# A two-block network on one NeuronCore: branch products over four PSUM banks, and the 96-slot expert pass written in line

## The reference

```python
def gated_mixer(h, w_in, ...):
    proj = h @ w_in
    gates = jax.nn.sigmoid(proj[..., o0:] + b_gate).reshape(B, S, 2, D)
    out_a = diff_attention(qa, ka, va, lam, lam_init, subln_w)
    out_b = chunk_band_attention(qb, kb, vb, rel_bias)
    merged = gates[:, :, 0] * (out_a @ w_branch_a) + gates[:, :, 1] * (out_b @ w_branch_b)
    return merged @ w_out

def moe_ffn(h, w_router, b_router, w_exp_in, b_exp_in, w_exp_out, b_exp_out):
    logits = t @ w_router + b_router
    top_val, top_idx = lax.top_k(logits, TOP_K)          # 4 of 32 experts per token
    gate_w = jax.nn.softmax(top_val, axis=-1)
    # for each expert, on the tokens that chose it:
        hb = xb @ w_exp_in[e] + b_exp_in[e]
        g = jnp.minimum(hb[:, :D_FF_2], 7.0); u = jnp.clip(hb[:, D_FF_2:], -7.0, 7.0)
        a = g * jax.nn.sigmoid(1.702 * g) * (u + 1.0)
        y = a @ w_exp_out[e] + b_exp_out[e]
```

## Time and profile before

| | before |
|---|---|
| median of three runs | 1506.52 us |
| profiled execution: device time | 1507.34 us |
| profiled execution: span, first to last instruction | 1505.5 us |
| around the span | 1.84 us |
| PE busy | 1339.8 us (89%) |
| VectorE busy | 448.4 us (30%) |
| ScalarE busy | 359.8 us (24%) |
| instructions executed | 25303 |

### The profile page before, as it was taken

One profiled execution on the slowest core, in us unless ns is written; L12 is line 12 of the kernel. 1 busy time (PEld: TensorE's weight loads), 2 busy tenths in 40 slices (PEclk: granted clock), 3 DMA queues, 4 the chain that ended last, 5 costly groups with the idle time before them and its releaser, 6 DMA issues.

```text
span 1505.5 us, 25303 instructions
## 1 busy us (share of the span) xinstructions
PE 1339.8 (89%) x9344; PEld 801.1 (53%) x9345; DVE 448.4 (30%) x906; ACT 359.8 (24%) x690; POOL 139.0 (9%) x65
## 2 busy tenths in 40 slices
PE   7999999998999898988998888998889988889865
PEld 6454999887989863434343333343334333433432
DVE  1326677745543771111111111111011111111112
ACT  1234666545566520101000100010001001000101
POOL 0000122005765400000000000000000000000000
PEclk9999999999999999999999999999999999999997
DMA  9442466855344478999999999999999999999996
GB/s 342 152 129 56 118 190 181 320 195 187 135 147 168 168 285 364 429 425 427 424 411 426 429 426 426 424 412 425 427 424 428 411 425 426 428 428 424 407 427 258
DMA packets 113493, 494.35 MB, mean 328 GB/s; under 512 B 7617, under 2 KB 55089, under 8 KB 80465
## 3 DMA queue, kind: packets, MB, share of 16 engines
q1 hardware_dynamic: 111971, 491.50, 81.5%
q10 hardware_dynamic: 1486, 2.34, 0.4%
HBM read 492.76 MB, written 1.06 MB: 328 GB/s over the span
## 4 chain that ended last, share of the span: by engine, by line
PE 59%; DMA 33%; DVE 3%; ACT 2%; issue 2%; SPq 0%; DVEq 0%; ACTq 0%
DMA big_mem<-in_w_exp_in 29%; PE ps L953 16%; PE ps L994 6%; PE ps L696 5%; PE ps L698 5%; PE ps L697 5%; PE ps L524 4%; PE ps L936 4%; DMA big_mem<-in_w_exp_out 3%; PE ps L668 2%; PE ps L720 1%; PE ps L722 1%; PE ps L721 1%; PE ps L1017 1%; PE ps L513 1%
## 5 line engine op out<-in xcount | busy, mean ns | idle before, releaser
L953 PE MATMUL ps<-big_mem,ring_mem 128*32 128x512 f32 (+1 forms) x2304 | 382.4, 640 | 67.7 <-DMA big_mem<-in_w_exp_in 67.7
L953 PEld LDWEIGHTS ps<-big_mem,ring_mem 128*32 128x32 f32 (+1 forms) x2304 | 112.6, 125 | 313.2 <-issue 200.8
L994 PE MATMUL ps<-big_mem,x 128*32 128x256 f32 (+1 forms) x1888 | 181.9, 430 | 8.3 <-DMA big_mem<-in_w_exp_out 4.5
L696 PE MATMUL ps<-hT_hi,w_hi 128*128 128x256 f32 x600 | 171.2, 285 | 1.3 <-DVE hT_lo L1619 1.3
L936 PEld LDWEIGHTS ps<-ring_mem,h 128*128 128x128 f32 x1056 | 137.3, 200 | 62.5 <-issue 61.3
L698 PE MATMUL ps<-hT_hi,w_lo 128*128 128x256 f32 x600 | 169.8, 283 | 0.0
L697 PE MATMUL ps<-hT_lo,w_hi 128*128 128x256 f32 x600 | 169.8, 283 | 0.0
L936 PE MATMUL ps<-ring_mem,h 128*128 128x96 f32 x1056 | 154.7, 291 | 0.9 <-DVE ring_mem L2040 0.9
L2081 DVE TENSOR_SCALAR ring_mem<-ps 128x256 f32<-128x256 f32 (+1 forms) x36 | 18.7, 520 | 429.9 <-PE ps L953 429.9
L1524 ACT ACTIVATE ring_mem<-ring_mem 128x256 f32<-128x256 f32 (+1 forms) x36 | 17.7, 493 | 492.0 <-DVE ring_mem L2081 492.0
L994 PEld LDWEIGHTS ps<-big_mem,x 128*32 128x32 f32 (+1 forms) x1888 | 70.6, 115 | 105.8 <-issue 64.7
(11 more groups left out here) (335 smaller groups left out, 1465.2 us busy)
## 6 DMA issues: line engine op xcount, KB each, us to landing
big_mem<-in_w_exp_in SPq DMA_DIRECT2D x128, 2048.0 KB, 22.7
big_mem<-in_w_exp_out SPq DMA_DIRECT2D x128, 1024.0 KB, 22.5
ring_mem<-in_w_in SPq DMA_DIRECT2D x15, 2048.0 KB, 8.0
ring_mem<-in_w_up SPq DMA_DIRECT2D x44, 512.0 KB, 5.0
ring_mem<-in_w_down SPq DMA_DIRECT2D x5, 2048.0 KB, 8.7
ring_mem<-in_w_out SPq DMA_DIRECT2D x4, 2048.0 KB, 8.1
ring_mem<-in_w_branch_a SPq DMA_DIRECT2D x1, 2048.0 KB, 7.5
ring_mem<-in_w_branch_b SPq DMA_DIRECT2D x1, 2048.0 KB, 7.6
```

The source lines that it names most:

```text
L696: mm(out, hi, x_hi, start=start, stop=False)
L953: last = mm(out, stationary, weights[:, f, w * q:w * (q + 1)] if m > XS else weights[:, :, w * q:w * (q + 1)], start=start, stop=stop)
L994: last = mm(ps[m * q:m * (q + 1), 4 + at // XS, 0:w], aT[:, k % n, k // n, :], wout[:, k, w * q:w * (q + 1)], start=(k == 0), stop=(k == K ...
```

## The change

Three things change, all of them on PE's list, with the reads of the moved banks on ScalarE and VectorE following.

- Block m goes to bank m % 4. Steps i = 2 and 3 wait for block m - 4 to be merged, steps i = 0 and 1 for none. The transposes of `oD` go to banks 4 and 5, and wait for `pv_out` instead of `proj_act`. `closing` now waits until block 4 has been merged before it writes bank 0.
- The first pass of a 96-slot expert is written in line. The inner loop follows it, over turns 1 and 2, and is entered only if `more` is above 0.
- A pass of 96 slots no longer waits at its start for the whole gathered input (the wait is for 2, a count passed before the first expert); the wait before its sixth step stays.

```diff
+        def merge_bank(m):
+            return m % 4
...
-            pe.wait_ge(s["proj_act"], 31)
+            pe.wait_ge(s["pv_out"], 11)
             pe.wait_ge(s["oD_ready"], 1)
             for hd in range(4):
                 for t in range(T):
-                    last = nc.tensor.transpose(ps[:, hd // 2, ...
+                    last = nc.tensor.transpose(ps[:, 4 + hd // 2, ...
...
-                        if m >= 2 and side == 0:
-                            pe.wait_ge(s["merged_ready"], m - 1)
+                        if i >= 2 and side == 0:
+                            pe.wait_ge(s["merged_ready"], m - 3)
...
-                            last = three(ps[:, 2 + z, SEQ * side:SEQ * (side + 1)], ...
+                            last = three(ps[:, merge_bank(m), SEQ * side:SEQ * (side + 1)], ...
...
+                pe.wait_ge(s["merged_ready"], 5)
                 closing(q, 0)
                 pe.wait_ge(s["merged_ready"], KD - 1)
...
                 if len(blocks) > 1:
-                    pe.wait_ge(s["xT_ready"], tokens_all)
+                    pe.wait_ge(s["xT_ready"], 2)
...
                     with pe.If(extra > 1):
-                        with pe.Fori(0, PASSES) as p:
-                            with pe.If(more >= p):
-                                one_pass(GROUPS[2], landed_all, load_next)
+                        one_pass(GROUPS[2], landed_all, load_next)
+                        with pe.If(more > 0):
+                            with pe.Fori(1, PASSES) as p:
+                                with pe.If(more >= p):
+                                    one_pass(GROUPS[2], landed_all, load_next)
+                                pe.nop()
                             pe.nop()
                         pe.nop()
```

More of the change, by code:

```diff
@@ L826, in _ @@
                 for t in range(T):
-                    last = nc.tensor.transpose(ps[:, hd // 2, 256 * (hd % 2) + P * t:256 * (hd % 2) + P * (t + 1)],
+                    last = nc.tensor.transpose(ps[:, 4 + hd // 2, 256 * (hd % 2) + P * t:256 * (hd % 2) + P * (t + 1)],
                                                m2["oD"][:, t, P * hd:P * (hd + 1)], ident)
@@ L843, in _ @@
                             cut = slice(P * z, P * (z + 1))
-                            last = three(ps[:, 2 + z, SEQ * side:SEQ * (side + 1)], branch_split(branch_hi, p)[:, k, cut], branch_split(branch_lo, p)[:, k, cut],
+                            last = three(ps[:, merge_bank(m), SEQ * side:SEQ * (side + 1)], branch_split(branch_hi, p)[:, k, cut], branch_split(branch_lo, p)[:, k, cut],
                                          x_hi[:, k, :], x_lo[:, k, :], k == 0, k == 3)
@@ L1457, in _ @@
             for r in range(2):
-                run(oa_hi[:, 2 * r:2 * r + 2, :].rearrange("p a b -> p (a b)"), ps[:, r, :], ACT.Copy).then_inc(s["oa_hi"], 1)
+                run(oa_hi[:, 2 * r:2 * r + 2, :].rearrange("p a b -> p (a b)"), ps[:, 4 + r, :], ACT.Copy).then_inc(s["oa_hi"], 1)
             values(11)
@@ L1926, in merge @@
                 dve.wait_ge(s["branch_ps"], m + 1)
-                v.tensor_tensor(mergedT[:, m, :], ps[:, 2 + m % 2, 0:SEQ], m2["gateT"][:, m, :], ALU.mult)
-                link(v.tensor_tensor(m2["tmp"][:, m % 2, :], ps[:, 2 + m % 2, SEQ:2 * SEQ], m2["gateT"][:, KD + m, :], ALU.mult))
+                v.tensor_tensor(mergedT[:, m, :], ps[:, merge_bank(m), 0:SEQ], m2["gateT"][:, m, :], ALU.mult)
+                link(v.tensor_tensor(m2["tmp"][:, m % 2, :], ps[:, merge_bank(m), SEQ:2 * SEQ], m2["gateT"][:, KD + m, :], ALU.mult))
                 v.tensor_tensor(mergedT[:, m, :], mergedT[:, m, :], m2["tmp"][:, m % 2, :], ALU.add).then_inc(s["merged_ready"], 1)
@@ L1954, in _ @@
                 pair = slice(2 * r, 2 * r + 2)
-                v.tensor_tensor(oa_lo[:, pair, :].rearrange("p a b -> p (a b)"), ps[:, r, :],
+                v.tensor_tensor(oa_lo[:, pair, :].rearrange("p a b -> p (a b)"), ps[:, 4 + r, :],
                                 oa_hi[:, pair, :].rearrange("p a b -> p (a b)").bitcast(F32), ALU.subtract).then_inc(s["oa_lo"], 1)
```

## The result

The changed kernel takes 1542.53 us (median of four runs, 1539.6 to 1549.04), the kernel before 1507.14 in the same comparison. The ratio is 1.0244, with a 95% interval of 1.021 to 1.0278: 36.8 us slower (32 to 42). The two medians are 35.4 us apart. The forecast was 1532, with 1520 to 1556 for its own case.

A forecast was written before the change was run, and what follows sets the result against it. PE bounds the branch products, closing and the time just behind 96-slot passes; elsewhere PE waits for weights. Branch products -3.4 plus 4 x (5.1 + 4.0 - 1.9) = 28.8 gave +25.4, so 1532 us; stated range 1496 to 1552.

The forecast's parts named there:

- its own case: PE keeps only eight code pages, so each 96-slot expert has two misses; 1532 us, range 1520 to 1556, chance 0.56.
- ten pages or more: Faster rival: PE keeps ten code pages or more, or fetches in time; 1496.5 us, chance 0.28.
- lost once: Rival of about the same time: over eight pages stay, each lost once in the first 96-slot pass; 1501 us, 0.14.
- the fixed place: Far slower rival: a code page's place follows its number, so two collide in all experts; above 1552 us, chance 0.02.
- Part 1: Branch products: PE's four waits for `merge` go; -3.4 us, ends 1.5 and 4.65, passed on by `closing`.
- the prediction's rule: Branch products: GpSimd contends with VectorE instructions of two SBUF inputs; alone, merges stay slow and the gain is 1.5 us.
- Part 2: Fewer branch instructions around 96-slot passes: entry -0.5 us, exit -1.4, together -1.9 us of PE per 96-slot expert.
- The wait: Start of a 96-slot pass: dropping the wait for the whole gathered input is worth 0.
- filling the dips: Weight-rate dips behind the four 96-slot passes nearly all fill with less PE time before them: -6.6 us, ends 0 and -7.1.
- Part 3: Second copy makes PE miss code pages behind each 96-slot pass: 5.1 + 4.0 us in each of four experts.
- The second one: Jump back to the head of the experts' loop misses its page: 4.0 us per 96-slot expert, ends 1.1 and 5.07.
- The first: Jump over the second copy misses the page of the loop's end: 5.07 us per 96-slot expert.

The follow-up runs named there:

- e5: e3 with 204 instructions at the start of PE's list that are jumped over, moving the loop against the page boundaries; 1547.06 us, ratio 1.0268.
- e10: Changed kernel, full second copy kept, with one back-edge hint instruction added at the head of the loop over experts; 1506.66 us, ratio 0.9991.
- e1: Kernel before with only the branch-product banks changed (four banks, oD transposed into banks 4 and 5), experts' code as before; 1505.16 us, ratio 0.9986.
- e4: Changed kernel with one copy of the 96-slot body in a loop of more + 1 turns, serving all inputs; 1501.76 us, ratio 0.9959.
- e12: e4 with the branch products of the kernel before, so without the four banks; 1503.85 us, ratio 0.9979.
- e2: Changed kernel without the second copy of the 96-slot body; the in-line pass stays, further passes are left out; 1503.26 us, ratio 0.9978.
- e8: e4 with the old wait for the whole gathered input at a 96-slot pass's start; 1502.21 us, ratio 0.9967.
- e9: Changed kernel with the never-run code twice as long, the inner loop holding the 96-slot body twice; 1541.96 us, ratio 1.0246.
- e3: Changed kernel with the second copy shortened to the input product gu, about 276 instructions in place of 625; 1502.02 us, ratio 0.9953.
- e7: Kernel before with only the experts' part of the change, branch products as before; 1546.55 us, ratio 1.0264.
- e6: e4 with some 52 instructions at the start of PE's list that are jumped over; 1499.04 us, ratio 0.9948.

## Why the prediction was right

**The case.** It forecast eight pages kept, and two stalls behind each 96-slot pass that come when the weights' lead is used up. The packets, the two long branches at each of the four places, the windows, e5 and e10 show that. The sign held, and so did the case's own range of 1520 to 1556; the stated range of 1496 to 1552 takes in the faster rival too and says less. The forecast was 10 us too low. Of the rivals, "ten pages or more" and "lost once" fail by the packets in all four 96-slot experts, and the fixed place by the experts between them, with no packet from 835 to 943 us.

**Part 1, -3.4.** It measured -3.2 to the end of `closing`, the `oD` wait 0 (14.15 us from the last scores at 470.66 to the transposes before, 14.16 after), and the new bound is the merge, 2.07 us. The merges beside GpSimd's products stayed slow, as the prediction's rule had it (2.04 and 1.85 us after; the same merge beside GpSimd's memsets took 0.42), but that did not hold the gain at 1.5 us. That it passes unhindered to the end was optimistic: in the profiled execution of the changed kernel nothing of it was left at 721 us, and by e1, and e4 against e12, 2 to 3 us reach the end. The prediction did not see that the jump into the first body meets its code by a narrow margin (0.10 us of idle time in the kernel before, 0.28 in e2, 0.82 in e1, 2.22 in the changed kernel, 3.03 in e4), and that the clock falls behind the longer gaps.

**Part 2, -1.9 for each 96-slot expert.** The entry gave -0.4 for -0.5. The exit, seen in e4 where no stall hides it, gave 1.77 - 0.24 = 1.5 for 1.4. The wait was worth nothing (e8). That filling the dips brings 6.6 us was too much: e12, which has this part alone (by the counted loop, with the same way out as e4), is 3.2 us faster than the kernel before (0.9 to 5.4), and e4 against e1 is 0.0027 in ratio, 4 us.

**Part 3, +9.1 for each.** This is the term that was mis-sized. The way out without stalls is 0.24 us and with them 11.57: the stalls cost 11.3. The second one was put at 4.0, and the branch took 4.7 to 5.3, so 4.8 more than the usual 0.21 on the mean. The first was put at 5.1, and its branch took 5.9 to 7.0, so 6.4 more. The 5.07 us seen before were what was left of a branch of 6.06 us (L1088 at 583.08): the sequencer came to it 2.5 us ahead of the end of PE's last matmul, so part of the stall was hidden by PE's own work. Behind a 96-slot pass it comes only 1.1 us ahead. What also goes with a long branch is the packet just ahead of it, for the page behind the copy. Where that one came during the branch, 1 us ahead of the missing page's, the branch took 6.8 to 7.0 us; where it had come 3 us earlier (979.9 against 983.2), 5.9. e9 has the same pair, 6.7 and 6.8 against 6.1 and 6.2. With 11.3 in place of 9.1 the sum is 4 x (11.3 - 1.9) - 3.2 = +34.4, and 36.8 was measured.

**The count of pages.** The prediction put the kernel before at eight and the changed one at ten. It is seven and nine: the head of the loop lay just on the other side of a boundary. That the forecast came out alike is luck: nine is too many as well. Had the second copy been 350 instructions shorter, the same reasoning would have forecast a loss where e3 shows none.

**The Trainium skill** (Runtime: NRT & Kernel Launch, "Instruction fetch mechanics") was cited for 2048 instructions in blocks of 256 on PE. e3 and e10 on one side and e5 and the changed kernel on the other agree with that. The same section's "only 2 cache lines" does not hold for PE here: e10 runs and jumps about in eight pages for 735 us without a packet.

## What to carry to other kernels

Code that never runs is not free where it stands inside a hot loop: count the pages that a run through the loop touches, from page boundary to page boundary and with one page ahead of each stretch, against the eight that PE kept here, before copying a body. In a profile the sign is idle time put down to "issue" at the same branch in every turn, with packets on that engine's instruction queue beside it. A loop with a counted number of turns (e4) gave the gain of the in-line copy without the copy.

## What was not expected of the hardware

A branch to a page that was gone took 4.5 to 7.1 us behind the 96-slot passes of the changed kernel, e5, e7 and e9, and 7.7 us once in e6, against 0.21 us with the page there. The shortest was 3.63 us, in e5 at 551 us, when the DMA engines were nearly idle (0.04 of their time). The 2.17 us at 550 us in the changed kernel were for a page that had been asked for ahead. Where code lies was worth more than the change itself: 204 never-run instructions at the start of the program moved the time by 45 us (e3 to e5), and one hint instruction took 36 us away (the changed kernel to e10). Behind a gap of 11 to 12 us PE's granted clock in the 20-us windows was 0.71 to 0.74; behind 1.8 us it was 0.91, and in the same windows without a gap 1.00.
